# A hybrid attention decoder step: residual loaded by quarters, operand jobs moved by some slots, four transpose banks, memory tokens in eight transfers

## The reference, cut to what matters

```python
m = rms_norm(mem_prompt, g_mem_norm)              # 256 x 2048
kv = einsum('bmd,de->bme', m, w_mem_kv)           # memory keys and values
hp = rms_norm(x_prompt, g_norm)                   # 512 x 2048
qd, kd, vd, gd, qw, kw, vw, gw, qm, gm = split(hp @ w_in)
od, ow, om = diff_attn(...), dilated(...), memory_attn(qm, mk, mv)
cat = concat([rms_norm(od) * silu(gd), ow * silu(gw), om * silu(gm)])
y = rms_norm(x_prompt + cat @ w_out, g_final)
```

## Time and profile before

| what | value |
|---|---|
| median of 3 runs | 1031.95 us (1031.47 to 1033.26) |
| the profiled execution's own time | 1031.1 us |
| its span in the profile | 1029.3 us |
| TensorE busy | 97% of the span |
| VectorE busy | 71% |
| ScalarE busy | 43% |
| DMA, mean | 198 GB/s |

### The profile page before, as it was taken

One profiled execution on the slowest core, in us unless ns is written; L12 is line 12 of the kernel. 1 busy time (PEld: TensorE's weight loads), 2 busy tenths in 40 slices (PEclk: granted clock), 3 DMA queues, 4 the chain that ended last, 5 costly groups with the idle time before them and its releaser, 6 DMA issues. The chain is left out here.

```text
span 1029.3 us, 24065 instructions
## 1 busy us (share of the span) xinstructions
PE 1001.1 (97%) x8079; PEld 979.1 (95%) x8079; DVE 735.3 (71%) x2708; ACT 444.6 (43%) x1174; POOL 54.2 (5%) x122
## 2 busy tenths in 40 slices
PE   6999999999999999999999999999999999999995
PEld 6999999999999999999999999999999999999995
DVE  5783267777888777778777667577774697788874
ACT  5763222223333333444433544225665365555552
POOL 0200000000000000000000000000001000000002
PEclk9999999999999999999999999999999999999998
DMA  9863289987978877776775686997753325433224
GB/s 298 247 195 107 64 265 255 290 288 218 271 223 248 266 238 222 219 229 200 235 217 171 191 262 173 250 284 245 213 167 106 116 71 195 122 104 104 83 83 166
DMA packets 254521, 203.31 MB, mean 198 GB/s; under 512 B 12481, under 2 KB 207671, under 8 KB 253751
## 3 DMA queue, kind: packets, MB, share of 16 engines
q1 hardware_dynamic: 253934, 200.67, 65.3%
q10 hardware_dynamic: 464, 1.12, 0.3%
HBM read 189.98 MB, written 11.76 MB: 196 GB/s over the span
## 5 line engine op out<-in xcount | busy, mean ns | idle before, releaser
L1088 PE MATMUL z<-act_hi,w_hi 128*128 128x260 f32 (+1 forms) x1984 | 428.9, 292 | 2.5 <-DVE act_lo L2136 2.0
L1088 PE MATMUL z<-act_hi,w_lo 128*128 128x260 f32 (+1 forms) x1984 | 410.1, 283 | 0.0
L1088 PE MATMUL z<-act_lo,w_hi 128*128 128x260 f32 (+1 forms) x1984 | 409.4, 283 | 0.0
L1088 PEld LDWEIGHTS z<-act_hi,w_hi 128*128 128x128 f32 x1984 | 312.3, 189 | 7.9 <-issue 5.4
L1088 PEld LDWEIGHTS z<-act_lo,w_hi 128*128 128x128 f32 x1984 | 310.7, 189 | 0.0
L1088 PEld LDWEIGHTS z<-act_hi,w_lo 128*128 128x128 f32 x1984 | 310.3, 189 | 0.0
L1668 DVE TENSOR_TENSOR w_lo<-w_raw,w_hi 128x512 fp32r<-128x512 f32 x300 | 205.8, 688 | 120.6 <-ACT w_hi L1342 119.5
L1342 ACT ACTIVATE w_hi<-w_raw 128x512 fp32r<-128x512 f32 x300 | 185.3, 625 | 189.3 <-PE z L1088 162.1
L1857 DVE CUSTOM_DVE_ANT_0 pages<-pages,q_bc 128x128 f32<-128x128 f32 x640 | 144.3, 286 | 24.7 <-DMA pages<-in_cache_k_win_dram 12.7
L1886 DVE SCALAR_TENSOR_TENSOR v_acc<-pages,dec_a,v_acc 128x256 f32<-128x256 f32 x224 | 94.3, 477 | 2.2 <-DMA pages<-in_cache_v_diff_dram 2.1
L1464 ACT ACTIVATE probs<-probs,st_n 128x128 f32<-128x128 f32 (+3 forms) x48 | 26.8, 558 | 79.9 <-DVE st_n L1796 79.5
(11 more groups left out here) (232 smaller groups left out, 1161.7 us busy)
## 6 DMA issues: line engine op xcount, KB each, us to landing
w_raw<-in_w_in_dram SPq DMA_DIRECT2D x224, 256.0 KB, 4.4
pages<-in_cache_k_diff_dram SPq DMA_DIRECT2D x128, 256.0 KB, 4.9
pages<-in_cache_v_diff_dram SPq DMA_DIRECT2D x128, 256.0 KB, 3.5
w_raw<-in_w_out_dram SPq DMA_DIRECT2D x64, 256.0 KB, 2.8
w_raw<-in_w_mem_kv_dram SPq DMA_DIRECT2D x32, 256.0 KB, 6.2
cat<-in_x_prompt_dram SPq DMA_DIRECT2D x8, 1024.0 KB, 7.8
q_bc<-q_rows_dram SPq DMA_DIRECT2D x32, 256.0 KB, 6.6
pages<-in_cache_mem_k_dram SPq DMA_DIRECT2D x16, 256.0 KB, 6.8
```

What stands on the lines that cost most here:

```text
L1088: last = nc.tensor.matmul(zb[:, bank, 0:b - a], lhs[:, w], rhs[:, kt, a:b], start=(kt == 0 and m == 0), stop=(kt == KT - 1 and m == 2))
```

## The change

The memory tokens come in eight transfers of 256 columns, with eight semaphores, and the weight loads stand between them otherwise. The preps of the memory tokens use four PSUM banks, two of them the second banks of `z`. The first weight splits stand after preps 0, 2, 4, 6, 7. The memory's `rstd` moves from slot 9 to 10, and the first two evacuations and their transposes by one slot. The last K block of the heads is split one slot later than the others of its group, in slot 257; operand sum 6 moves from slot 254 to 257, split 1 from 253 to 258, and splits 3 and 4 by one slot. The residual is loaded in slots 259, 276, 302 and 330, 1 MB each. The transpose of y tile 12, the first of the last pair, moves from slot 347 to 348.

```diff
-FIRST_SPLITS = (0, 1, 2, 4, 6)
+FIRST_SPLITS = (0, 2, 4, 6, 7)
...
     if e > LAST_PAIRED - 2:
-        return DONE[n] + (3 if e % 2 else 1)
+        return DONE[n] + (3 if e % 2 else 2)
...
-T_ADDS = ((2, -11), (0, -10), (1, -9), (4, -8), (5, -7), (3, -4), (6, -2), (7, 1))
+T_ADDS = ((2, -11), (0, -10), (1, -9), (4, -8), (5, -7), (3, -4), (6, 1), (7, 1))
...
-T_SPLIT_AT = (-4, -3, 2, 2, 3, 4, 6, 8)
+T_SPLIT_AT = (-4, 2, 2, 3, 4, 4, 6, 8)
+HEADS_AT = ((0, 1, 2, 3), (4, 5, 6, 7), (8, 9, 10, 11), (12, 13, 14), (15,))
+RESIDUAL_AT = (3, 20, 46, 74)
...
-    put(9, "mem", "rstd")
+    put(10, "mem", "rstd")
...
-            put(s + (6, 3)[n] if n < 2 else s, "evac", n, 0.65 if kind in ("gd", "gw") else 1.3 if kind == "gm" else 0.0)
+            put(s + (7, 4)[n] if n < 2 else s, "evac", n, 0.65 if kind in ("gd", "gw") else 1.3 if kind == "gm" else 0.0)
...
-            put(s + (7, 5)[n] if n < 2 else s + (2 if n < FIRST_IN else 1), "nat", n)
+            put(s + (8, 6)[n] if n < 2 else s + (2 if n < FIRST_IN else 1), "nat", n)
...
-                cols = slice(512 * i, 512 * (i + 1))
+                cols = slice(256 * i, 256 * (i + 1))
                 sp.dma_start(nat[:, 0:2, cols], m_t.rearrange("t p f -> p t f")[:, :, cols]).then_inc(s_mtok[i], 16)
-            memory_chunk(0)
-            memory_chunk(1)
+            for i in range(3):
+                memory_chunk(i)
             weights(0)
+            memory_chunk(3)
             weights(1)
             for i in range(2, 4):
-                memory_chunk(i)
+                memory_chunk(2 * i)
+                memory_chunk(2 * i + 1)
                 weights(i)
...
-                if s == IN_END + 3:
-                    sp.wait_ge(s_tadd, len(T_ADDS))
-                    sp.wait_ge(s_clo, KT)
-                    for i in range(4):
-                        cols = slice(512 * i, 512 * (i + 1))
-                        sp.dma_start(nat[:, :, cols], x_t.rearrange("t p f -> p t f")[:, :, cols]).then_inc(s_res[i], 16)
+                if s - IN_END in RESIDUAL_AT:
+                    i = RESIDUAL_AT.index(s - IN_END)
+                    if i == 0:
+                        sp.wait_ge(s_tadd, len(T_ADDS))
+                        sp.wait_ge(s_clo, KT)
+                    cols = slice(512 * i, 512 * (i + 1))
+                    sp.dma_start(nat[:, :, cols], x_t.rearrange("t p f -> p t f")[:, :, cols]).then_inc(s_res[i], 16)
...
+        def prep_bank(use):
+            if use < N_PREP:
+                return (s_ps[:, 0, :], s_ps[:, 1, :], z[0][:, 1, :], z[1][:, 1, :])[use % 4]
+            return s_ps[:, use % 2, :]
...
-                    pe.wait_ge(s_mtok[u // 2], 16)
-                if use >= 2:
-                    pe.wait_ge(s_plo, use - 1)
+                    pe.wait_ge(s_mtok[u], 16)
+                if use >= (4 if use < N_PREP else 2):
+                    pe.wait_ge(s_plo, use - (3 if use < N_PREP else 1))
...
-                if IN_END - 3 <= s <= IN_END:
-                    for kt in range(4 * (s - IN_END + 3), 4 * (s - IN_END + 3) + 4):
+                if IN_END - 3 <= s <= IN_END + 1:
+                    for kt in HEADS_AT[s - (IN_END - 3)]:
                         dve.wait_ge(s_chi, kt + 1)
                         nc.vector.tensor_tensor(act_lo[:, kt, :], cat_t[:, kt, :], act_hi[:, kt, :].bitcast(F32),
                                                 ALU.subtract).then_inc(s_clo, 1)
```

More of the change, by code:

```diff
@@ L642, in hybrid_decoder @@
         s_gm = sem("g_mem_loaded")
-        s_mtok = [sem(f"memory_loaded{i}") for i in range(4)]
+        s_mtok = [sem(f"memory_loaded{i}") for i in range(N_PREP)]
         s_tok = [sem(f"tokens_loaded{i}") for i in range(7)]
@@ L1018, in prep @@
                         kt = 2 * u + k
-                        last = nc.tensor.transpose(s_ps[:, use % 2, (2 * k + t) * P:(2 * k + t + 1) * P],
+                        last = nc.tensor.transpose(prep_bank(use)[:, (2 * k + t) * P:(2 * k + t + 1) * P],
                                                    nat[:, first + t, kt * P:(kt + 1) * P], ident[:, :])
@@ L1317, in squares @@
                 else:
-                    for chunk in range(4):
+                    for chunk in range(N_PREP):
                         act.wait_ge(s_mtok[chunk], 16)
@@ L1330, in prep_hi @@
                     kt = 2 * u + k
-                    last = nc.scalar.activation(act_hi[:, kt, first:first + 2 * P], s_ps[:, use % 2, k * 2 * P:(k + 1) * 2 * P],
+                    last = nc.scalar.activation(act_hi[:, kt, first:first + 2 * P], prep_bank(use)[:, k * 2 * P:(k + 1) * 2 * P],
                                                 ACT.Identity, scale=g[:, kt:kt + 1])
@@ L1582, in slot @@
                         act.wait_ge(s_fin, 3)
-                    r = s - (IN_END - 3)
-                    act.wait_ge(s_quarter, IN_END - 3 + r)
-                    for kt in range(4 * r, 4 * r + 4):
+                    act.wait_ge(s_quarter, min(s, IN_END))
+                    for kt in HEADS_AT[s - (IN_END - 3)]:
                         if kt >= 3 * H:
@@ L1620, in prep_lo @@
                     cols = slice(first, first + 2 * P)
-                    last = nc.vector.scalar_tensor_tensor(act_lo[:, kt, cols], s_ps[:, use % 2, k * 2 * P:(k + 1) * 2 * P],
+                    last = nc.vector.scalar_tensor_tensor(act_lo[:, kt, cols], prep_bank(use)[:, k * 2 * P:(k + 1) * 2 * P],
                                                           g[:, kt:kt + 1], act_hi[:, kt, cols].bitcast(F32), ALU.mult, ALU.subtract)
```

## The result

The changed kernel takes 1039.22 us (median of 6 runs, 1037.64 to 1040.26) against 1031.82 for the kernel before beside it: 1.0069 times, 95% interval 1.0057 to 1.0082. It is slower by some 7 us, where 1.2 were forecast, and above the range. The profiled execution, from which all rows of it are read, is the slowest of the six: 1040.26 us with a span of 1038.5.

The account below looks back on a forecast made before the run. The prediction took TensorE, 97% busy, to bound the kernel. Its seven terms, -1.2 + 2.0 + 0.9 - 4.6 + 3.6 - 0.8 + 1.3, gave +1.2 us: a median of 1033.1 us, range 1029.8 to 1036.0.

Parts of the forecast that it names:

- Step 1: Start of the kernel: four banks let the preps follow at once, -1.2 us; later landing of transfers taken as 0.
- Step 2: Slot 10: the memory's rstd one slot later delays the diagonal, +2.0 us; moved evacuations and transposes cost nothing.
- Step 3: Heads, slots 256 to 263: last act_lo later, one 3.4 us wait at q259, none at q257, +0.9 us.
- Step 4: First pair: with 1 MB of residual instead of four transfers it becomes like the other pairs, -4.6 us.
- Step 5: Residual quarters in slots 302 and 330 delay the loads of q309 and q337, 1.8 us a time, +3.6 us.
- Rival A: Slower: residual quarters land late, each costing 3.0 to 3.2 us instead of 1.8; +2.6 us, 1035.7; chance 0.17.
- Step 6: Last pair: y tile 12 transposed one slot later, so a quarter covers TensorE's wait for it, -0.8 us.
- Step 7: TensorE's clock falls once, behind the longer new idle time (3.4 us, at the heads), +1.3 us.
- Rival B: Slower: the clock falls at both stalls, behind slot 10 too; +1.3 us, 1034.4; chance 0.16.

Follow-up runs that it names:

- e5: Changed kernel with rstd, first evacuations and transposes, heads and operand jobs in their old slots, residual quarters in slots 304 and 332: 1028.43 us.
- e7: Kernel before with only the residual by quarters (slots 259, 276, 304, 332) and y tile 12's transpose one slot later: 1025.67 us.
- e6: e5 with the memory tokens in four transfers instead of eight, four banks kept: 1025.81 us.
- e15: e8 with the two banks and first weight splits of the kernel before: 1023.71 us.
- e8: e6 with the changed kernel's heads and operand jobs, but operand sums 6 and 7 in slot 258 instead of 257: 1024.43 us.
- e1: Changed kernel with rstd back in slot 9 and the first two evacuations and transposes in their old slots: 1035.87 us.
- e3: Changed kernel with the third and fourth residual quarters in slots 304 and 332 instead of 302 and 330: 1035.03 us.
- e4: Changed kernel with the heads in four groups of four, operand sum 6 and the operand splits in their old slots: 1036.06 us.
- e2: Changed kernel with the memory tokens in four transfers instead of eight, four banks kept: 1037.92 us.
- e9: e2 with rstd alone back in slot 9, the first evacuations and transposes staying one slot later: 1034.84 us.
- e10: e2 with the transpose of tile 1 one slot earlier, rstd staying in slot 10: 1038.45 us.
- e14: e10 with the memory-key stores issued on ScalarE's queue instead of SyncE's: 1037.52 us.
- e11: Kernel before with the eight memory-token transfers alone: 1032.44 us.
- e12: e8 with eight transfers again and weight loads 7 to 10 issued ahead of the two 1 MB token blocks: 1026.84 us.
- e13: Changed kernel with its whole start as in the kernel before; heads, operand jobs, residual quarters and y tile 12 stay changed: 1033.11 us.

## Why the prediction was wrong, step by step

**Step 1 failed, and with it the forecast.** "I take 0: no wait of TensorE in this stretch names a weight load" was the inference that did not hold. e5 and e7 differ by step 1 alone: 1028.43 against 1025.67, a loss of 2.8 us where a gain of 1.2 was forecast. e6 (1025.81) puts it on the eight transfers: with four transfers, four banks gain nothing that can be told (e6 against e7, e15 against e8).

In the changed kernel's trace TensorE gained more than was said: q0 came at 9.50 at full rate (the bound named for that case was 2.5 us; q3 came 3.32 earlier). But the load that nobody waited for had 3.06 us of slack, it was issued 1.23 us later (the four more issues did not lie under the full queue), and the later landing that stood there as a bound (0 to 1.6 us; 2.13 measured) was taken as 0 beside a TensorE that was made faster in the same step. All of the gain was gone at q8, and the clock with it.

That is one execution. e1, e3, e4 and e5 have the same start up to slot 8, and the same sum gives the wait in each (us; q6, q8 and q16 against the kernel before, load 7 by ScalarE's split of it):

| run | q6 earlier | load 7 later | 3.06 less both | q7 waited | q8 late by | q16 late by |
|---|---|---|---|---|---|---|
| after | 3.34 | 2.13 | -2.41 | 2.38 | 0.32 | 6.59 |
| e1 | 3.07 | 2.19 | -2.20 | 2.18 | -0.83 | 1.36 |
| e3 | 1.20 | 1.34 | 0.52 | 0 | -1.20 | 5.64 |
| e4 | 1.55 | 2.84 | -1.33 | 1.31 | 1.03 | 6.44 |
| e5 | 2.86 | 1.96 | -1.76 | 1.73 | -1.06 | 1.52 |

So the mechanism holds, but q7's own wait is not the whole price: in e3 q7 did not wait and q8 came 1.20 us earlier, just as forecast, and q16 was late all the same, by the diagonal (2.85), a stretch at half rate behind it and `k_nat` (1.39). In e1 and e5, with `rstd` back in slot 9, the gain is lost between q8 and q16.

**Step 2 was right as far as it went.** The gap in front of `r_diag`'s multiplication is 2.63 us (2.5 said). In e2's trace, where no load is late and the rate holds, TensorE loses 1.99 us from q8 to q11 (2.0 said). In the medians it is more: 3.1 us by e9 against e2, and 3.35 by e1, which takes the whole step back. Its last sentence failed: the moved evacuations and transposes were not "nothing". In e9, where they alone are left of the step, the wait on `k_nat` is 2.17; in e6, where they are back too, 0.12. Late loads bring that wait as well: 0.98 and 1.34 in e1 and e5, which have eight transfers and the old slots. In all it is 0.98 us or more in e1 to e5, e9, e10 and e14, 0.49 in e11, and at most 0.13 in e6, e8, e12, e13 and e15.

**Step 3 was right.** q259 came 0.92 us later than the lateness it inherited (0.92 said), after 3.33 us of idle time (3.4 said); none at q257. e4 confirms it.

**Step 4 was right**: the first pair took 21.58 us and gave 4.18 (4.6 said).

**Step 5 was right in mechanism and too small.** The split of q309 began 937.45 - 934.03 = 3.42 us into its pair, and 930.11 - 928.95 = 1.16 before: 2.26 us later (2.0 said). TensorE then waits three times in the pair, and the pair loses 2.41 (1.8 said); e13 loses 2.70 and 2.38 in the two pairs against e15, which has the same start and the later slots. 3.6 was forecast, 4.2 (e3) to 5.1 measured. Rival A's point of 2.3 us a time was reached, so its direction held, at half its price.

**Step 6 was right**: the 0.75 us gap is gone, and in e7 the stretch from q334 to q363 is 0.79 us shorter (0.8 said).

**Step 7 counted one fall of the clock; there were three**, behind idle times of 2.38, 2.63 and 3.33 us. The last one cost 1.53 us at q259 (1.3 said). Rival B, that slot 10 brings one too, happened in this execution, beside one nobody had named, at q7.

**The sum.** Of the 5.9 us missed by the ratios (7.1 against 1.2), 4.7 are the start (5.5 against 0.8), the rest mostly step 5. By the medians step 1 missed by 4.0 (e5 against e7) and step 2 by 1.35 (the changed kernel against e1). The range could not hold this: with the whole gain of step 1 gone and rival B besides, the forecast's own sum is +3.7 us. That step 1 could turn into a loss was not among the bounds.

## What to carry to other kernels

A wait that isn't in the list of waits is not a resource with room: before speeding up an engine, read for each of its inputs how long it lay ready (here 3.06 us), and subtract the speed-up and the delay together. When a change both hurries the consumer and adds work to the producer's queue, take the bound, not 0. And put late work behind the last thing the next stage waits for: moving the two sums by one slot (e8) and the quarters by two (e3) turned both parts from losses into gains.

## What the runs showed of the hardware

The fall of TensorE's clock did not follow from the length of one idle time. It fell behind 3.33 us in the changed kernel; in its profiled execution e9 has the same wait at the same place and held:

```profile
847.51 0.48 PE L1097 MATMUL z<-act_hi,w_hi 128*128 128x260 f32 x2 [3.34 <-DVE act_lo L2144]
...
847.50:853.50 6.00, 5.99 (x50) 6.00 (x51) 5.79 (x7) 4.62 (x7) 0.76 (x1) 1.00 0.73 244
```

In e2 it held behind 2.72 us, where TensorE worked on at full rate; in e10 it fell behind the same 2.72 us at the same place, and in e4 at a wait of 1.31:

```profile
35.14:41.10 5.96, 5.96 (x46) 5.73 (x47) 3.34 (x11) 3.48 (x7) 2.59 (x3) 1.00 0.73 192
```

```profile
35.76 1.22 PE L1270 MATMUL o_ps<-r_diag,ones 128*128 128x256 f32 x2 [2.72 <-DVE r_diag L2066]
...
35.76:38.97 3.21, 3.21 (x13) 3.03 (x14) 1.36 (x3) 0.00 (x0) 0.00 (x0) 0.50 1.00 248
```

```profile
27.29 0.58 PE L1099 MATMUL z<-act_hi,w_hi 128*128 128x256 f32 x1 [1.31 <-DVE w_lo L1678]
...
27.20:30.60 3.40, 3.31 (x15) 3.31 (x16) 3.19 (x5) 3.40 (x7) 0.05 (x1) 0.51 1.17 288
```

It also differs between executions of one kernel. Of e3's ten, the two with the highest mean granted clock (0.995) took 1031.17 and 1031.44 us, the others (0.989 to 0.994) 1033.64 to 1035.90; of e9's seven, the profiled one (0.997) took 1031.62, the others (0.991 to 0.995) 1033.01 to 1035.78. So a stall of 1.3 to 3.3 us is to be priced with a fall and without: at q259 the two are 1.5 to 2.4 us apart (the changed kernel, e1, e2, e3, e10, e13 and e14 against e9). The rule of the Trainium skill that step 7 named, "TensorE: Matmul & The Clock Gate", section "Why this matters for your kernels", that a long idle time between bursts puts the clock back, agrees with the changed kernel's 3.33 us; e9 and e4 show that the length of one idle time alone does not decide. What else does was not tried.

The rate at the start differs too: from q0 to q1 is 2.30 us in the changed kernel and 3.88 before, as the clock had risen before q0 in the one and not in the other (the matmuls of q0 take 0.28 us against 0.42). The change does not settle this: in the twelve profiles with four banks the stretch is 2.29 or 2.30 us in six and 3.87 to 4.26 in the other six, e3 and e4 among them, whose start is that of the changed kernel; in the five with two banks it is 3.34 to 3.89.
